# First block's attention with scores three heads ahead, four score banks, two transpose banks, two value banks and three weight buffers

## The reference, cut to what matters

```
for l in range(DEPTH):                      # DEPTH = 2
    h = rms_norm(x, norm_mix[l]);  z = h @ w_in[l]
    ...                                     # split z; norm and rotate q_a, k_a
    s = einsum("bqhgd,bkhd->bhgqk", q_blk, k) * ATT_SCALE
    p = softmax(s)                          # over the 256 keys
    o_att = einsum("bhgqk,bkhd->bqhgd", p, v)
    mix = concatenate([o_att, o_hg, o_cv])  # recurrence and convolution beside it
    x = x + mix @ w_out[l]
    x = x + square(relu(rms_norm(x, norm_mlp[l]) @ w_mlp_in[l])) @ w_mlp_out[l]
```

## Time and profile before

| what | value |
|---|---|
| median of three runs | 3020.66 us |
| the profiled execution's own time | 3021.48 us |
| its span in the profile | 3019.7 us |
| PE busy | 2788.3 us (92%) |
| DVE busy | 1822.0 us (60%) |
| ACT busy | 1291.6 us (43%) |
| share of PE in the chain that ended last | 85% |

### The profile page before, as it was taken

The page is one execution under the profiler, slowest core; times in us unless marked ns, Lnnn a source line. Parts: engine busy times, 40 slices in busy tenths (PEclk is TensorE's granted clock), DMA queues, the critical chain, the costliest instruction groups (busy, mean ns, idle before and its releaser), DMA issues.

```text
span 3019.7 us, 44886 instructions
## 1 busy us (share of the span) xinstructions
PE 2788.3 (92%) x18124; PEld 2488.9 (82%) x18124; DVE 1822.0 (60%) x3066; ACT 1291.6 (43%) x1473; POOL 154.3 (5%) x74
## 2 busy tenths in 40 slices
PE   7888999788999799999999999897898999999998
PEld 6756988648978499899999988786898899999886
DVE  4774645755544379964555566655699845555565
ACT  4434534434434345444444444343454444444443
POOL 1000001000000060000000000000420000000000
PEclk9988999879999799999999999998999999999999
DMA  6201554103554143565556567431435655656672
GB/s 248 112 1 57 183 194 151 56 1 131 190 186 142 46 166 140 201 254 188 207 209 215 208 230 275 177 137 70 143 139 196 240 193 210 221 196 219 223 266 97
DMA packets 72888, 507.15 MB, mean 168 GB/s; under 512 B 8096, under 2 KB 8368, under 8 KB 18096
## 3 DMA queue, kind: packets, MB, share of 16 engines
q1 hardware_dynamic: 58576, 424.70, 39.2%
q10 hardware_dynamic: 5472, 47.03, 3.9%
q0 software_dynamic: 8704, 33.56, 3.1%
HBM read 467.51 MB, written 37.75 MB: 167 GB/s over the span
## 4 chain that ended last, share of the span: by engine, by line
PE 85%; DVE 10%; issue 2%; ACT 2%; DMA 1%; ACTq 0%; DVEq 0%
PE lin L1345 16%; PE lin L1346 16%; PE lin L1347 16%; PE m L1345 8%; PE m L1346 8%; PE m L1347 8%; PE m L1702 4%; PE m L1452 2%; DVE lo L768 2%; PE m L1445 1%; PE m L1430 1%; DVE st L934 1%; PE m L1407 1%; PE m L1518 1%; PE m L1340 1%
## 5 line engine op out<-in xcount | busy, mean ns | idle before, releaser
L768 DVE TENSOR_TENSOR lo<-raw,hi 128x2048 fp32r<-128x2048 f32 x381 | 872.1, 2294 | 731.6 <-ACT hi L391 723.4
L1345 PE MATMUL lin<-xh,hi 128*128 128x256 f32 x3408 | 981.4, 288 | 22.0 <-DVE lo L768 11.1
L391 ACT ACTIVATE hi<-raw 128x2048 fp32r<-128x2048 f32 x403 | 769.3, 1910 | 502.9 <-PE m L1347 343.0
L1346 PE MATMUL lin<-xl,hi 128*128 128x256 f32 x3408 | 970.7, 285 | 0.0
L1347 PE MATMUL lin<-xh,lo 128*128 128x256 f32 x3408 | 970.4, 285 | 0.0
L1345 PEld LDWEIGHTS lin<-xh,hi 128*128 128x128 f32 x3408 | 661.0, 194 | 30.6 <-DVE lo L768 18.6
L1346 PEld LDWEIGHTS lin<-xl,hi 128*128 128x128 f32 x3408 | 660.9, 194 | 4.4 <-issue 1.2
L1347 PEld LDWEIGHTS lin<-xh,lo 128*128 128x128 f32 x3408 | 660.2, 194 | 0.0
L1345 PE MATMUL m<-hi,ah 128*128 128x512 f32 x1024 | 399.7, 390 | 0.0
L1346 PE MATMUL m<-lo,ah 128*128 128x512 f32 x1024 | 399.1, 390 | 0.0
L1347 PE MATMUL m<-hi,al 128*128 128x512 f32 x1024 | 398.4, 389 | 0.0
(11 more groups left out here) (304 smaller groups left out, 2744.9 us busy)
## 6 DMA issues: line engine op xcount, KB each, us to landing
raw<-stream SPq DMA_DIRECT2D x403, 1024.0 KB, 4.8
gate_table<-stg ACTq DMA_DIRECT2D x16, 2048.0 KB, 6.4
g<-gate_table POOLq DMA_DIRECT2D x32, 1024.0 KB, 8.4
rows<-rows ACTq DMA_DIRECT2D x4, 1024.0 KB, 7.5
x_scratch<-x ACTq DMA_DIRECT2D x2, 1024.0 KB, 4.2
x<-x_scratch ACTq DMA_DIRECT2D x2, 1024.0 KB, 7.3
x<-mem SPq DMA_DIRECT2D x1, 1024.0 KB, 7.4
x<-x ACTq DMA_DIRECT2D x1, 1024.0 KB, 11.4
```

The costliest lines, as they stand in the source:

```text
L391: act.activation(HI[i % SLOTS][:], RAW[:, i % SLOTS, :], ACT.Copy).then_inc(hi_ready, 1)
L768: dve.tensor_tensor(LO[i % SLOTS][:], RAW[:, i % SLOTS, :], HI[i % SLOTS][:].bitcast(F32), ALU.subtract).then_inc(lo_ready, 1)
L1345: pe.matmul(out_, ah, bh, start=first, stop=False, **kw)
L1346: pe.matmul(out_, ah, bl, start=False, stop=False, **kw)
```

## The change

Three new functions take the place of the calls in the first block: `eight_heads_pe`, `eight_heads_act` and `eight_heads_dve`. The second block keeps the old ones. The arithmetic, the number of instructions and their shapes are the same.

- Scores of head n go to bank `SB[n % 4]` (`M[0]`, `M[1]`, `PS[0]`, `PS[3]`), turned weights to `TB2[n % 2]` (`PS[1]`, `M[2]`), values to `OB2[n % 2]` (`PS[2]`, `M[3]`). The buffer `PM` has three places instead of two.
- PE issues scores 0, 1 and 2 and turn(0), then for each n: scores(n + 3), turn(n + 1), values(n).
- DVE issues head_max 0, 1 and 2, then for each n: head_scale(n), head_max(n + 3), between(n).
- ACT issues the exponentials of heads 0 and 1, then for each n: the copy of the turned weights of n, the exponentials of n + 2, the copy of the values of n - 1, between(n).
- The waits follow: scores(n) wait for the exponentials of n - 4 instead of n - 2, turn(n) for the copy of n - 2 instead of n - 1, values(n) for the copy of n - 2 instead of n - 1. PE waits for `crs_ready` and `hrs_ready` ahead of turn(0), because the banks `PS[1]` and `PS[2]` are read before these.

```diff
-        PM = at("pm", [P, 2, 2, TOK], off=r1)
-        PT = at("pt", [P, 2, 2, TOK], off=r1 + 4096)
+        PM = at("pm", [P, 3, 2, TOK], off=r1)
+        PT = at("pt", [P, 2, 2, TOK], off=r1 + 6144)
...
+        SB, TB2, OB2 = [M[0], M[1], PS[0], PS[3]], [PS[1], M[2]], [PS[2], M[3]]
...
+        def eight_heads_act(act, a, l, between):
...
+            exps(0)
+            exps(1)
+            for n in range(8):
+                g = 8 * l + n
+                act.wait_ge(sem("pt_done"), g + 1)
+                if n >= 2:
+                    act.wait_ge(sem("pv_done"), g - 1)
+                a.mark(act.activation(flat(PT[:, n % 2, :, :]), TB2[n % 2][:], ACT.Copy), sem("pt_ready"))
+                if n + 2 < 8:
+                    exps(n + 2)
+                if n >= 1:
+                    out_(n - 1)
+                between(n)
+            out_(7)
...
+        def eight_heads_dve(dve, v, l, between):
+            scale = HEAD ** -0.5
+
+            def head_max(n):
+                c = 16 + 8 * (n % 4)
+                dve.wait_ge(sem("sc_done"), 8 * l + n + 1)
...
+            def head_scale(n):
+                c = 16 + 8 * (n % 4)
+                dve.wait_ge(sem("exp_ready"), 8 * l + n + 1)
...
+            for n in range(3):
+                head_max(n)
+            for n in range(8):
+                head_scale(n)
+                if n + 3 < 8:
+                    head_max(n + 3)
+                between(n)
...
+            def eight_heads_pe(l):
+
+                def scores(n):
+                    part, g = slice(64 * (n // 4), 64 * (n // 4) + 64), 8 * l + n
+                    if n >= 4:
+                        pe.wait_ge(sem("exp_ready"), g - 3)
...
+                def turn(n):
+                    g = 8 * l + n
+                    pe.wait_ge(sem("sm_ready"), g + 1)
+                    if n >= 2:
+                        pe.wait_ge(sem("pt_ready"), g - 1)
...
+                for n in range(3):
+                    scores(n)
+                pe.wait_ge(sem("crs_ready"), l + 1)
+                pe.wait_ge(sem("hrs_ready"), l + 1)
+                turn(0)
+                for n in range(8):
+                    g, o = 8 * l + n, 64 * (n // 4)
+                    if n + 3 < 8:
+                        scores(n + 3)
+                    if n + 1 < 8:
+                        turn(n + 1)
+                    pe.wait_ge(sem("pt_ready"), g + 1)
+                    if n >= 2:
+                        pe.wait_ge(sem("o_ready"), g - 1)
...
```

More of the change, by code:

```diff
@@ L349, in _, with exps, out_ @@
             sp.wait_ge(sem("out_stored"), 16)
+        def eight_heads_act(act, a, l, between):
+            def exps(n):
+                g = 8 * l + n
+                c = 16 + 8 * (n % 4)
+                act.wait_ge(sem("nb_ready"), g + 1)
+                if n >= 3:
+                    act.wait_ge(sem("pt_done"), g - 2)
+                for qt in range(2):
+                    ins = act.activation(PM[:, n % 3, qt, :], SB[n % 4][:, 256 * qt:256 * qt + 256], ACT.Exp, scale=HEAD ** -0.5,
+                                         bias=SMALL[:, c + 2 + qt:c + 3 + qt], accum_out=SMALL[:, c + 4 + qt:c + 5 + qt])
+                a.mark(ins, sem("exp_ready"))
+            def out_(n):
+                act.wait_ge(sem("pv_done"), 8 * l + n + 1)
+                o = 64 * (n // 4)
+                a.mark(act.activation(MIXF[o:o + 64, n % 4, :], OB2[n % 2][o:o + 64, 0:256], ACT.Copy), sem("o_ready"))
+            exps(0)
[12 more added lines that the diff above has]
+            out_(7)
+            act.wait_ge(sem("o_ready"), 8 * l + 8)
         def attention_act(act, a, g0, heads, scale, dst, part, PM=PM, PT=PT, between=lambda n: None, panel=lambda n: None):
@@ L733, in _ @@
                 rstd(SMALL[:, 60:62], SMALL[:, 56:60].rearrange("p (t k) -> p t k", k=2)[:, :, 1], 1, LN_EPS, sem("ln_rstd"))
+        def eight_heads_dve(dve, v, l, between):
[3 more added lines that the diff above has]
+                dve.wait_ge(sem("sc_done"), 8 * l + n + 1)
+                v.step(dve.tensor_reduce(SMALL[:, c:c + 2], SB[n % 4][:].rearrange("p (q k) -> p q k", q=2), AX.X, ALU.max))
+                v.step(dve.tensor_scalar(SMALL[:, c + 2:c + 4], SMALL[:, c:c + 2], -scale, None, ALU.mult), sem("nb_ready"))
+            def head_scale(n):
+                c = 16 + 8 * (n % 4)
+                dve.wait_ge(sem("exp_ready"), 8 * l + n + 1)
+                v.step(dve.reciprocal(SMALL[:, c + 6:c + 8], SMALL[:, c + 4:c + 6]))
+                for qt in range(2):
+                    ins = dve.tensor_scalar(PM[:, n % 3, qt, :], PM[:, n % 3, qt, :], SMALL[:, c + 6 + qt:c + 7 + qt], None, ALU.mult)
+                v.step(ins, sem("sm_ready"))
+            for n in range(3):
[5 more added lines that the diff above has]
+                between(n)
         def attention_dve(dve, v, g0, heads, scale, PM=PM, between=lambda n: None):
@@ L998, in _ @@
                 lo_to(h0 + N_IN + N_OUT)
-                attention_dve(dve, v, 8 * l, 8, HEAD ** -0.5, between=other_outputs)
+                eight_heads_dve(dve, v, l, other_outputs)
                 mix_low(0, 4, 2 * l + 2)
@@ L1399, in wide @@
                 ins.then_inc(hp_used, 1)
+            def eight_heads_pe(l):
[3 more added lines that the diff above has]
+                        pe.wait_ge(sem("exp_ready"), g - 3)
+                    for qt in range(2):
+                        ins = pe.matmul(SB[n % 4][:, 256 * qt:256 * qt + 256], QK[part, n % 4, P * qt:P * qt + P], QK[part, 4, :], start=True, stop=True)
+                    ins.then_inc(sem("sc_done"), 1)
+                def turn(n):
+                    g = 8 * l + n
+                    pe.wait_ge(sem("sm_ready"), g + 1)
+                    if n >= 2:
+                        pe.wait_ge(sem("pt_ready"), g - 1)
+                    for kt in range(2):
+                        for qt in range(2):
+                            ins = pe.transpose(TB2[n % 2][:, 256 * kt + P * qt:256 * kt + P * qt + P], PM[:, n % 3, qt, P * kt:P * kt + P], cst("ident"))
+                    ins.then_inc(sem("pt_done"), 1)
+                for n in range(3):
[12 more added lines that the diff above has]
+                        pe.wait_ge(sem("o_ready"), g - 1)
+                    for kt in range(2):
+                        ins = pe.matmul(OB2[n % 2][o:o + 64, 0:256], VA[:, kt, o:o + 64], PT[:, n % 2, kt, :], start=(kt == 0), stop=(kt == 1))
+                    ins.then_inc(sem("pv_done"), 1)
+                pe.wait_ge(sem("o_ready"), 8 * l + 7)
             def attention_pe(g0, heads, q, k, val, part, PM=PM, PT=PT, panel=lambda n: None):
@@ L1536, in _ @@
                 pe.wait_ge(sem("qk_ready"), l + 1)
[L1537 to L1539 removed]
+                eight_heads_pe(l)
                 pe.wait_ge(sem("mixl_ready"), 2 * l + 1)
```

3 lines of the change are left out of this document (1 added, 2 removed).

## The result

The changed kernel takes 3040.99 us (median of 4 runs, 3039.51 to 3042.74) against 3020.78 for the kernel before: the ratio is 1.0069, with a 95% interval of 1.0051 to 1.0086. It is slower, by some 20 us. The profiled execution took 3042.74 us at a span of 3040.9 us.

What follows compares the result with a forecast made beforehand. Each attention stage was taken as bound by a turn, scores, reduction, scaling ring: 17.7 us more at the low clock, less 4.0, makes 13.7, twice 27.4; on 3021.48 that is 3048.9, 3048 for the median, range 3036 to 3056.

Steps and rivals of the forecast that it cites:

- What bounds the stage: Attention stage before the change: at the full clock a ring of turn, scores, maximum, scaling, 3.61 us; level with PE at 5.03 low.
- The order on DVE and PE together: Between turns, values, scores, reduction, DVE's other work and scaling stand in one line; the other work adds 4.3 us.
- The ring at the low clock: Turn to turn in the changed stage: 7.01 us against 5.03 before; at the full clock 4.62 against 3.61.
- The start: Stage start: the reduction of head 2 stands ahead of head_scale(0), so turn(0) comes at 221.94 instead of 220.47.
- the other bound (5.02): Stage start: turn(0) at 220.99 if the clock still holds for the scores of head 2.
- Which clock: Stage: rings at the low level, a rise about half-way through the tail saving 2.6 us; the stage costs 13.7 us more.
- their 1.4 us: First panels behind each stage: begun at the full clock, seven of their matmuls give back 1.4 us.
- the low-clock sum: Whole stage at the low clock: turn(1) at 226.97, turn(5) at 259.31, panels at 270.4, 17.7 us later than before.
- ACT and the buffers: Stage: ACT's 19.6 us hides under the ring; the third weight buffer and extra banks remove waits that don't end last.
- The run-ahead working: Rival for the stages: PE bound by itself, gaining about 9 us a layer, 3003 us; chance 3%.
- The clock staying up: Rival for the stages: the full-clock sum holds, -0.9 us a layer, 3019 to 3023 us; chance 5%.
- The clock coming back early: Rival: last two rings, whole tail and panels at the full level, 6.2 us more a layer, 3034 us; chance 12%.

Runs made afterwards that it cites:

- e5: Changed kernel with DVE's other work ahead of the reduction and PE in the order turn(n), scores(n + 3), values(n); 3022.07 us, ratio 0.9997 to the kernel before.
- e1: Changed kernel with DVE scaling head n + 1 ahead of the reduction of head n + 3; 2998.17 us, ratio 0.9938 to the kernel before.
- e2: Changed kernel with DVE's other work of step n ahead of the reduction of head n + 3; 3032.42 us, ratio 1.0043 to the kernel before.
- e4: Changed kernel with two extra matmuls on constants behind the scores of n + 3, for n = 0 to 4; 3029.27 us, ratio 1.0034 to the kernel before.
- e3: Changed kernel with PE back in the order turn(n), scores(n + 3), values(n); 3025.53 us, ratio 1.0022 to the kernel before.
- e9: e1 with three score banks instead of four and two weight buffers instead of three; 2999.45 us, ratio 0.9945 to the kernel before.
- e11: Kernel before, scores two ahead, with DVE scaling head n + 1 ahead of the reduction of head n + 2; 3024.44 us, ratio 1.0015.
- e12: e11 with ACT's copy of the turned weights of n ahead of the exponentials of n + 2, other work last; 3024.96 us, ratio 1.0014 to the kernel before.
- e7: e1 with one bank for turned weights and one for values instead of two of each; 3005.58 us, ratio 0.9966 to the kernel before.
- e10: Kernel before with four extra matmuls on constants in PE's gap between scores(1) and turn(0); 3024.71 us, ratio 1.0016.

## Why the prediction was right, and where its size was off

*What bounds the stage* was read rightly: the ring of turn, scores, reduction, scaling at the full clock. e5 has its 3.6 us again, and in e1 two turns come as close as 2.65 us, PE's own work.

*The order on DVE and PE together.* Right. The gaps stand ahead of turn(1) to turn(5) and are ended by the scaling, and DVE's wait for scores is 22.6 us (about 25 was forecast). The ring at the low clock was put at 7.01 us and measured 6.93 in e2; at the full clock 4.62 against 4.63 in e4. Undoing either the place of the values (e3) or of DVE's other work (e2) takes its part away, and undoing the queueing itself (e1) takes the whole loss and more.

*The start.* I took the low-clock figure, turn(0) 5.97 us after the first scores. It came after 4.99, which is the other bound (5.02): the clock still held for scores(2). A term too large by 1.0 us.

*Which clock.* This is the step that was mis-sized: "I take the rings at the low level and a rise about half-way through this tail". The tail took 8.28 us against 11.07 at the low level, so 2.8 less where I took 2.6, and the panels began at the full clock and gave back their 1.4 us, as put. But the clock was up three more times before. The windows view of the changed kernel, cut where the level changes:

```profile
216.77:223.20 6.43, 4.30 (x19) 3.29 (x20) 3.37 (x9) 5.15 (x15) 0.00 (x0) 0.95 0.00 0
223.20:229.00 5.80, 3.89 (x11) 1.73 (x9) 1.64 (x5) 2.24 (x9) 0.00 (x0) 0.50 0.00 0
229.00:233.00 4.00, 1.32 (x5) 0.81 (x4) 2.44 (x5) 0.38 (x1) 0.00 (x0) 0.93 0.01 2
233.00:246.40 13.40, 7.96 (x21) 4.09 (x21) 4.87 (x14) 3.40 (x11) 0.00 (x0) 0.50 0.00 0
246.40:250.00 3.60, 1.69 (x9) 1.09 (x8) 1.65 (x5) 2.15 (x4) 0.00 (x0) 0.97 0.00 0
250.00:260.00 10.00, 8.09 (x21) 4.11 (x20) 3.90 (x12) 3.78 (x12) 0.00 (x0) 0.50 0.00 0
260.00:264.29 4.29, 3.71 (x18) 1.84 (x17) 1.23 (x1) 3.01 (x5) 0.00 (x0) 0.99 0.00 0
```

It was near full speed for 6.4 us at the start, for 4.0 around the scores of head 4, and for 3.6 around those of head 6. Against the low-clock sum turn(1) came 0.7 us sooner, and the four rings behind it took 0.9, 0.1, 1.0 and 0.4 us less: 3.1 us, and 4.1 with the start. I had argued that only an unbroken run of some 11 us brings the clock back. But the earlier trace rows held a second rise, near 255.7, that I read and didn't use: PE had then worked without a gap only since this line of the kernel before, 5 us:

```profile
250.78 1.97 PE L1430 MATMUL m<-pt,va 128*64 128x256 f32 x4 [0.69 <-ACT pt L356]
```

In the changed kernel it came back, at 229.4 and at 246.4, when PE had worked for some 3 us (a turn, the values, a first piece of the scores) since gaps of 1.91 and 3.72 us. The length of the unbroken run alone doesn't decide it either, since 4.98 us of one, from turn(2) on, brought nothing:

```profile
234.72:239.70 4.98, 4.98 (x12) 2.62 (x12) 0.00 (x0) 1.89 (x6) 0.00 (x0) 0.50 0.00 0
```

What does decide it, these runs don't show.

So a stage cost 10.7 us instead of 15.1 before the panels give back their 1.4. The whole came to 20 us where I had forecast 27. Two errors worked against each other in it: the two stages grew by 8.8 us less than forecast (21.4 instead of 30.2), while the stretches outside them, which I took as unchanged but for the panels, grew by 2.6 us.

*ACT and the buffers.* ACT hid, as forecast. That the extra banks and the third buffer "remove waits that don't end last" holds for the changed kernel, whose gaps on PE in the rings are all ended by DVE's scaling, and e9 shows it for the fourth score bank and the third weight buffer even in e1. It would be wrong to take from it that the lead is worth nothing: once the scaling is moved, the kernels with two heads of lead take 39 us a stage (e11, e12) and those with three 28 to 32 (e1, e7, e9), with the reservation made at e12.

*The rivals.* The run-ahead working was put at 3003 us; the kernel in which it works (e1) took 2998. It failed as a forecast of this change because of the place of the scaling of head n + 1 in DVE's program. The clock staying up was put at 3019 to 3023. e4 could hold it for half a stage only, and came to 3029. The clock coming back early was put at 3034, with the last two rings and the whole tail at the full clock. It came about in part: the measured 3041 lies halfway between it and the forecast.

## What to carry to other kernels

Running ahead pays only if every in-order engine on the way has the older item's work ahead of the newer item's: list the program of each engine for one period, and look for an instruction that waits for something which can't be issued until an instruction queued behind it has run. When a pipeline gets deeper, move the consumer of the old item in front of the producer of the new one, here the scaling of n + 1 in front of the maximum of n + 3; that reorder turned 20 us of loss into about 20 of gain. The same reorder with two heads of lead gained nothing (e11, e12: 5 us slower), so try it together with the deeper lead and not instead of it. Then take away buffers again, since the version that scales first ran as fast with one bank and one buffer less.

## What the runs showed of the hardware that I had not expected

The granted clock moves stages whose code did not change. The six matmuls with `rot` ahead of the second attention (line 1518 before, 1618 in e1) are the same instructions on the same shapes. First the kernel before, then e1, each from PE's timeline:

```profile
632.49 4.63 PE L1518 MATMUL m<-qk,cst 128*128 128x512 f32 x6
```

```profile
624.43 2.42 PE L1618 MATMUL m<-qk,cst 128*128 128x512 f32 x6
```

4.63 us at a granted clock of 0.50 against 2.42 at 1.00. Between the stages, with the same code, the profiled executions took 386.6 us (before), 382.3 (e1) and 385.7 (e7); behind the second stage 2343.7, 2346.0 and 2338.6. That is up to 7 us, a third of the effect under study. The executions of e1, e7 and e9 spread over 8 to 17 us and those of e5 over 14, where the kernel before spread over 3 to 7 beside each. This goes with the clock: four executions of e1 took 2996 to 2998 us at a mean granted clock of 0.962 or 0.963, one 3006 at 0.958 and one 3013 at 0.955. A difference of a few us between two of these kernels is therefore not shown here by their medians. In e10 the clock was held at one place and lost at another, with a worse sum.
